# Last residual of a two-layer decoder step: tiles 4 and 5 scaled and added on GpSimd, tile 3 on VectorE, six stores of the result

## The chip, the cores and the metric

One core of one Trainium2 chip. The metric is the device time of one execution, in microseconds; the median of three runs of the kernel before is 1430.1.

## The reference

The program is one inference step of a small decoder: 256 new prompt tokens and 8 x 8 sampled tokens, together 320 columns (TOK), go through two layers of 1024 channels. Each layer is a pair of half-step SwiGLU networks around a token mixer (gated delta rule in the first, latent attention in the second), with an RMSNorm before and after each of the six sub-layers. The change touches only the very end, the post-norm and the residual of the last sub-layer:

```python
x = x + 0.5 * rmsnorm(swiglu(rmsnorm(x, norm_pre[layer, 2]), ffn_in[layer, 1], ffn_out[layer, 1]), norm_post[layer, 2])
# rmsnorm: y * rsqrt(mean(y * y) + EPS) * g
```

and the store of that x, the outputs y_prompt and y_sample. Everything is float32.

## The kernel before

Activations lie transposed: channel on the partition, token on the free axis. The 1024 channels are KT = 8 tiles m of 128 x 320, each tile one slice `x[:, m, :]` of the residual (the profile calls it parx_sb) and one `y[:, m, :]`. Weights stream in as chunks, are split in a high and a low part by ScalarE (L263) and VectorE (L270), and TensorE multiplies all through the kernel. The order of work is written out by hand for each engine; engines wait for each other on counting semaphores.

The last sub-layer is stage s = 5. Its output product (L380 to L382) leaves tile m in PSUM bank m. What follows on each engine:

ScalarE (`post_act`, L389) squares every bank, and copies banks 1, 3 and 5, times the gain, to y (L392). VectorE (`post_dve_sum`, L482) sums the squares and copies banks 0, 2 and 4 to y (L495). Banks 6 and 7 stay in PSUM. TensorE sums over partitions with a matrix of ones, in two halves of 160 tokens, into banks 1 and 3 (L679 to L683). ScalarE makes the reciprocal root r_post from each half with Ln and Exp (L408, L410), and raises `rpost_ready` after each half.

Then comes the last residual, x + y * r_post, over four engines. VectorE (`last_residual_dve`, L438) scales tiles 0 and 1, and 2 and 3, by the first half of r_post, then the same by the second half; then it scales tiles 4 and 5 whole (one operation of 640 columns), adds them to x (640 columns), forms y for 6 and 7 out of PSUM, gain and r_post (L461), and adds these two tiles one by one (L447). TensorE (`last_sums_pe`, L427) adds tiles 0 to 3: it multiplies x by the identity into the bank (L433) and y by the identity on top (L436); for float32 each such product is two passes. ScalarE copies these four banks into x (L414).

The output y_t is stored in five pieces: ScalarE's queue issues tiles 0 and 1 (L417) and 2 and 3 (L419), SyncE's queue issues tiles 4 and 5, then 6, then 7 (L3035), each after the semaphore of its producer. SyncE then waits for all of them. GpSimd has nothing to do in this stage; the last it did was the products of the SwiGLU (`ffn_pool`, L837).

Of the kernel before, what the change touches and what calls it, by code (L numbers as in the profile page):

```python
# [32 lines left out]
TOK = SEQ + NSMP  # L33
KT = D_MODEL // P
# [89 lines left out]
def build(nc, io):  # L124
    ctx = ExitStack()
    with ctx:
# [4 lines left out]
        def sem(name):  # L131
            return ctx.enter_context(nc.semaphore(name))
# [8 lines left out]
        x = par_x[:, XOFF:XOFF + KT * TOK].rearrange("p (k t) -> p k t", k=KT)  # L141
# [5 lines left out]
        y = sb("y", [P, KT, TOK])  # L147
# [6 lines left out]
        r_post = sb("r_post", [P, TOK])  # L154
        r_pre = sb("r_pre", [P, TOK])
        gx = sb("gx", [P, TOK])
        HALF = [slice(0, TOK // 2), slice(TOK // 2, TOK)]
# [231 lines left out]
        def post_act(act, s, c_last, gcol):  # L389

            def copy(m):
                act.activation(y[:, m, :], bank[m][:, 0:TOK], ACT.Identity, scale=gcol(m)).then_inc(y_copied_act, 1)  # L392

            for m in range(KT):
                if m < KT - 1:
                    act.wait_ge(y_done, (KT - 1) * s + m + 1)
                else:
                    act.wait_ge(chunk_done, c_last + 1)
                if m >= 4:
                    act.wait_ge(y_summed, NSUM * s + max(1, m - 4))  # L400
                for t in (HALF if m == KT - 1 else [slice(0, TOK)]):
                    act.activation(sqx[m % 4][:, t], bank[m][:, t], ACT.Square).then_inc(y_squared, 1)
                if m in (1, 3, 5):
                    copy(m)
            for n, t in enumerate(HALF):
                st = STATS[f"post{s}"] - 1 + n
                act.wait_ge(stat_done, st)
                act.activation(r_post[:, t], bank[2 * n + 1][:, t], ACT.Ln, scale=1 / D_MODEL, bias=epsc[:, :]).then_inc(ln_done, 1)  # L408
                act.wait_ge(ln_done, st)
                act.activation(r_post[:, t], r_post[:, t], ACT.Exp, scale=-0.5).then_inc(rpost_ready, 1)  # L410
            if s == 5:
                for m in LAST_PE:
                    act.wait_ge(y_done, (KT - 1) * (s + 1) + LAST_PE.index(m) + 1)
                    act.activation(x[:, m, :], bank[m][:, 0:TOK], ACT.Copy).then_inc(y_copied_act, 1)  # L414
                    if m == LAST_PE[1]:
                        act.wait_ge(y_copied_act, 5 * s + 3 + 2)
                        act.dma_start(io["y_t"][:, 0:2, :], x[:, 0:2, :]).then_inc(third_then_out, 16)  # L417
                act.wait_ge(y_copied_act, 5 * s + 3 + 4)
                act.dma_start(io["y_t"][:, 2:4, :], x[:, 2:4, :]).then_inc(third_then_out, 16)  # L419
                return  # L420
            copy(6)
            copy(7)


        LAST_PE = (0, 1, 2, 3)

        def last_sums_pe(pe):  # L427
            s = 5
            pe.wait_ge(y_copied, 3 * (s + 1))
            for m in (0, 2, 1, 3):  # L430
                if m == 1:
                    pe.wait_ge(ln_done, STATS["post5"])
                pe.matmul(bank[m][:, 0:TOK], ident, x[:, m, :], start=True, stop=False)  # L433
            for m in LAST_PE:
                pe.wait_ge(y_scaled, (KT + 1) * s + (3 if m < 2 else 4))
                pe.matmul(bank[m][:, 0:TOK], ident, y[:, m, :], start=False, stop=True).then_inc(y_done, 1)  # L436

        def last_residual_dve(dve):  # L438
            s = 5
            gcol = half(5)  # L440
            wide = lambda t: r_post[:, t].unsqueeze(1).to_broadcast([P, 2, t.stop - t.start])

            def scale(m, t):
                dve.tensor_tensor(y[:, m:m + 2, t], y[:, m:m + 2, t], wide(t), ALU.mult).then_inc(y_scaled, 1)

            def add(lo, hi):
                dve.tensor_tensor(x[:, lo:hi, :], x[:, lo:hi, :], y[:, lo:hi, :], ALU.add).then_inc(x_ready, hi - lo)  # L447

            dve.wait_ge(y_copied, 3 * (s + 1))
            dve.wait_ge(y_copied_act, 5 * s + 3)  # L450
            dve.wait_ge(rpost_ready, 2 * s + 1)
            scale(0, HALF[0])
            scale(2, HALF[0])
            dve.wait_ge(rpost_ready, 2 * s + 2)
            scale(0, HALF[1])
            scale(2, HALF[1])
            scale(4, slice(0, TOK))
            dve.wait_ge(y_scaled, (KT + 1) * s + 5)
            add(4, 6)
            for m in (6, 7):  # L460
                dve.scalar_tensor_tensor(out=y[:, m, :], in0=bank[m][:, 0:TOK], scalar=gcol(m), in1=r_post[:, :],  # L461
                                         op0=ALU.mult, op1=ALU.mult).then_inc(y_scaled, 1)
            for m in (6, 7):
                dve.wait_ge(y_scaled, (KT + 1) * s + m)
                add(m, m + 1)

        def rsqrt_act(act, stat, n, out, inv_n, out_sem):

# [363 lines left out]
        def ffn_pool(pool, f):  # L832
            with pool.Fori(0, HT // 2) as j:
                for i in range(2):
                    pool.wait_ge(g_ready, HT * f + i + 1 + 2 * j)
                    pool.wait_ge(u_ready, HT * f + i + 1 + 2 * j)
                    pool.tensor_tensor(f_gu[i][:, :], f_g[i][:, :], f_u[i][:, :], ALU.mult).then_inc(gu_ready, 1)  # L837
# [140 lines left out]

        S0_AT = {(1, "d1"): ("keys", 0), (1, "d2"): ("keys", 1), (2, "d1"): ("queries", 0), (2, "d2"): ("queries", 1)}

        s0_landed, gate_copied = sem("s0_landed"), sem("gate_copied")
        gate_act, gate_dve, gate_pe, cols_ready = sem("gate_act"), sem("gate_dve"), sem("gate_pe"), sem("cols_ready")
        pre_ready, conv_first, conv_step, conv_exp = sem("pre_ready"), sem("conv_first"), sem("conv_step"), sem("conv_exp")
        silu_step, sig_ready, qkv_ready, pad_ready = sem("silu_step"), sem("sig_ready"), sem("qkv_ready"), sem("pad_ready")
# [2004 lines left out]
        @block.sync  # L2989
        def _(sp):  # L2990
            n1, n2 = XOFF + 2 * TOK, XOFF + 4 * TOK
            sp.dma_start(par_x[:, 0:n1], io["par_x"][:, 0:n1]).then_inc(x_landed, 16)
            sp.dma_start(par_x[:, n1:n2], io["par_x"][:, n1:n2]).then_inc(x_rest[0], 16)
            sp.dma_start(par_x[:, n2:], io["par_x"][:, n2:]).then_inc(x_rest[1], 16)
            for q in (2, 3):
                for c in range(2):
                    load_quarter(sp, c, q)
            sp.dma_start(raw_third[:, :], io["wts"][2, :, :]).then_inc(third_then_out, 16)
            sp.dma_start(con[:, :], io["consts"]).then_inc(con_landed, 16)
            sp.dma_start(pages[:, :], io["page_table"]).then_inc(con_landed, 16)  # L3000
            sp.dma_start(ctok_flat[:, 2 * KV_LORA - 64:], io["gw"]).then_inc(con_landed, 16)
            load_chunk(sp, 3)
            with sp.Fori(1, (BASE["uk"] - 2) // 2) as j:
                for i in range(2):
                    load_chunk(sp, 2 + i, j)
            load_chunk(sp, BASE["uk"] - 1)
            load_chunk(sp, BASE["uk"])
            sp.wait_ge(con_landed, 48)
            sp.wait_ge(chunk_done, BASE["dq"] + 2)
            load_pages(sp, 0, aland, 0)  # L3010
            load_pages(sp, 0, aland, 1)
            load_chunk(sp, BASE["uk"] + 1)
            sp.wait_ge(qn_hi, 4)
            sp.wait_ge(qn_lo, 4)
            sp.wait_ge(chunk_done, BASE["kv"] + 1)
            for i in range(2, NUN):
                load_pages(sp, 0, aland, i)
                load_plain(sp, 0, spland, i - 2)
            for i in range(NUN - 2, NUN):
                load_plain(sp, 0, spland, i)  # L3020
            sp.wait_ge(n_scores, NP)
            sp.wait_ge(s_done, NUN)
            sp.wait_ge(pv_page, QP * (NUN - 1))
            load_chunk(sp, BASE["uk"] + 2)
            sp.wait_ge(pv_page, QP * NUN)
            sp.wait_ge(s_ot, NP)
            load_chunk(sp, BASE["uk"] + 3)
            load_chunk(sp, BASE["uk"] + 4)
            c = BASE["uk"] + 5
            with sp.Fori(0, (NCHUNK - c) // 2) as j:  # L3030
                for i in range(2):
                    load_chunk(sp, c + i, j)
            for lo, hi in ((4, 6), (6, 7), (7, 8)):
                sp.wait_ge(x_ready, 5 * KT + hi - 4)
                sp.dma_start(io["y_t"][:, lo:hi, :], x[:, lo:hi, :]).then_inc(third_then_out, 16)  # L3035
            sp.wait_ge(third_then_out, 16 + 16 * 5)

        @block.gpsimd
        def _(pool):
# [37 lines left out]
                load_plain(pool, 1, ppland, i)  # L3077
            second_high_pool(pool, BASE["ffn3"] + 1)
            ffn_pool(pool, 3)
            pool.wait_ge(ss_out, 16 * NG)  # L3080
            pool.wait_ge(ss1_out, 16 * NG)
            pool.wait_ge(sp_out, 16 * NG)
# [202 lines left out]
```

## Time and profile before

| what | value |
|---|---|
| runs, median of 3 (lowest, highest) | 1430.1 us (1429.97, 1430.61) |
| profiled execution, span (the only time it gives) | 1428.4 us |
| TensorE busy | 1412.2 us, 99% |
| VectorE busy | 889.8 us, 62% |
| ScalarE busy | 742.7 us, 52% |
| GpSimd busy | 161.9 us, 11% |
| data moved by DMA | 221.01 MB, mean 155 GB/s |

The span runs from the first to the last instruction of the profiled execution. Busy shares are means over it; in the last residual TensorE and VectorE are both nearly always busy and GpSimd is idle. All times in the rows below are microseconds from the start of the span, unless marked ns. PE is TensorE, DVE VectorE, ACT ScalarE, POOL GpSimd, SP SyncE; a q behind the name is the engine's queue of DMA issues.

### The profile page before, as it was taken

How to read it: one execution, taken by the hardware profiler on the slowest of the kernel's cores; microseconds unless marked ns; L12 is line 12 of the kernel's file. 1: busy time of each engine (PE TensorE's matmuls, PEld its weight loads, DVE VectorE, ACT ScalarE, POOL GpSimd, SP SyncE). 2: the span in 40 equal slices, each digit the busy share in tenths (PEclk: the TensorE clock that was granted, in tenths of full speed). 3: DMA queues.
4: the chain of work that ended last, by engine and by line, in shares of the span. 5: the costliest groups of instructions: out<-in, count | busy, mean ns of one | idle time of the engine just before them, and what ended most of it. 6: DMA issues, size and time to landing. Idle time of an engine off the chain costs nothing.

```text
span 1428.4 us, 29450 instructions
## 1 busy us (share of the span) xinstructions
PE 1412.2 (99%) x11003; PEld 1346.2 (94%) x11003; DVE 889.8 (62%) x1480; ACT 742.7 (52%) x1218; POOL 161.9 (11%) x229
## 2 busy tenths in 40 slices
PE   9999999999999999999999999999999999999998
PEld 9999999999888999999999999999877699999998
DVE  6655535999888675554376555349755548655534
ACT  6555424788646565553265555346533346555423
POOL 0111000010110011110011111001144201111000
PEclk9999999999999999999999999999999999999999
DMA  6444443344242254444434444444599643444441
GB/s 242 163 149 151 153 154 136 119 152 146 100 155 98 89 177 147 147 147 148 147 119 166 154 151 147 154 147 150 187 293 285 212 156 118 169 152 150 147 147 67
DMA packets 50776, 221.01 MB, mean 155 GB/s; under 512 B 6705, under 2 KB 23474, under 8 KB 28802
## 3 DMA queue, kind: packets, MB, share of 16 engines
q1 hardware_dynamic: 38882, 189.07, 38.0%
q0 software_dynamic: 6192, 24.64, 5.2%
q10 hardware_dynamic: 5616, 6.16, 1.3%
q8 instruction: 54, 0.88, 0.3%
q14 instruction: 32, 0.26, 0.1%
HBM read 213.07 MB, written 6.77 MB: 154 GB/s over the span
## 4 chain that ended last, share of the span: by engine, by line
PE 94%; DVE 3%; ACT 2%; issue 1%; DMA 0%; DVEq 0%
PE psum L283 16%; PE psum L287 15%; PE psum L282 15%; PE psum L381 8%; PE psum L380 8%; PE psum L382 8%; PE psum L2681 2%; PE psum L2639 2%; PE psum L309 1%; PE psum L300 1%; PE psum L325 1%; PE psum L304 1%; PE psum L2510 1%; PE psum L311 1%; PE psum L315 1%; PE psum L1553 1%
## 5 line engine op out<-in xcount | busy, mean ns | idle before, releaser
L270 DVE TENSOR_TENSOR w_lo<-raw,w_hi 128x2048 fp32r<-128x2048 f32 x159 | 368.6, 2318 | 290.5 <-ACT w_hi L263 290.4
L263 ACT ACTIVATE w_hi<-raw 128x2048 fp32r<-128x2048 f32 x155 | 296.7, 1914 | 351.7 <-PE psum L382 207.8
L282 PE MATMUL psum<-h_hi,w_hi 128*128 128x320 f32 x1504 | 446.0, 310 | 0.0
L283 PE MATMUL psum<-h_lo,w_hi 128*128 128x320 f32 x1504 | 444.1, 309 | 0.0
L282 PEld LDWEIGHTS psum<-h_hi,w_hi 128*128 128x128 f32 x1504 | 282.1, 188 | 2.6 <-issue 1.3
L283 PEld LDWEIGHTS psum<-h_lo,w_hi 128*128 128x128 f32 x1504 | 283.4, 188 | 0.5
L287 PE MATMUL psum<-h_hi,w_lo 128*128 128x320 f32 x1504 | 251.3, 309 | 0.0
L287 PEld LDWEIGHTS psum<-h_hi,w_lo 128*128 128x128 f32 x1504 | 228.3, 188 | 0.3 <-DVE w_lo L270 0.3
L380 PE MATMUL psum<-hid_hi,w_hi 128*128 (+1 forms) x704 | 217.4, 309 | 0.0
L381 PE MATMUL psum<-hid_lo,w_hi 128*128 (+1 forms) x704 | 217.4, 309 | 0.0
L382 PE MATMUL psum<-hid_hi,w_lo 128*128 (+1 forms) x704 | 217.4, 309 | 0.0
L837 POOL TENSOR_TENSOR f_gu<-f_g,f_u 128x320 f32<-128x320 f32 x88 | 77.5, 881 | 567.1 <-DVE f_u L795 567.1
L380 PEld LDWEIGHTS psum<-hid_hi,w_hi 128*128 128x128 f32 x704 | 132.4, 188 | 0.0
L381 PEld LDWEIGHTS psum<-hid_lo,w_hi 128*128 128x128 f32 x704 | 132.4, 188 | 0.0
L382 PEld LDWEIGHTS psum<-hid_hi,w_lo 128*128 128x128 f32 x704 | 132.4, 188 | 0.0
L756 ACT ACTIVATE hid_hi<-f_h 128x320 f32 (+1 forms) x88 | 41.5, 472 | 128.1 <-DVE f_h L800 128.1
L794 DVE TENSOR_TENSOR f_g<-psum,r_pre 128x320 f32<-128x320 f32 x88 | 43.1, 490 | 72.2 <-PE psum L287 72.2
L803 DVE TENSOR_TENSOR hid_lo<-f_h,hid_hi 128x320 f32 (+1 forms) x88 | 43.3, 492 | 66.8 <-ACT hid_hi L756 66.8
L752 ACT ACTIVATE f_e<-f_e,onec 128x320 f32<-128x320 f32 x88 | 49.6, 563 | 2.9
L800 DVE TENSOR_TENSOR f_h<-f_gu,f_e 128x320 f32<-128x320 f32 x88 | 42.5, 483 | 5.0 <-ACT f_e L754 5.0
L480 POOL CAST w_hi<-raw 128x2048 fp32r<-128x2048 f32 x5 | 9.5, 1908 | 299.2 <-PE psum L382 299.2
L754 ACT ACTIVATE f_e<-f_e 128x320 f32<-128x320 f32 x88 | 41.6, 472 | 2.8
(459 smaller groups left out, 1957.4 us busy)
## 6 DMA issues: line engine op xcount, KB each, us to landing
raw<-wts SPq DMA_DIRECT2D x161, 1024.0 KB, 4.8
h_plain<-cache_t POOLq DMA_DIRECT2D x44, 160.0 KB, 3.7
h_plain<-cache_t SPq DMA_DIRECT2D x44, 160.0 KB, 3.7
arena<-s POOLq DMA_DIRECT2D x4, 1024.0 KB, 7.2
sgs<-arena POOLq DMA_DIRECT2D x4, 1024.0 KB, 4.6
marena<-cache_t POOLq DMA_DIRECT2D x20, 160.0 KB, 4.0
marena<-cache_t SPq DMA_DIRECT2D x20, 160.0 KB, 3.6
raw<-cache_c SPq DMA_DIRECT2D x16, 128.0 KB, 4.2
```

The costliest lines, as they stand in the source:

```text
L263: act.activation(w_hi[c0 % 2][:, :], raw_of(c0, pair)[:, :], ACT.Copy).then_inc(hi_ready, 1)
L270: eng.tensor_tensor(w_lo[c0 % 2][:, :], raw_of(c0, pair)[:, :], w_hi[c0 % 2][:, :].bitcast(F32), ALU.subtract).then_inc(lo_ready, 1)
L282: pe.matmul(outs[n], wtile(w_hi, c0, tile0 + n * K + k), src_hi(k), start=(k == 0), stop=False)
L283: pe.matmul(outs[n], wtile(w_hi, c0, tile0 + n * K + k), src_lo(k), start=False, stop=False)
L287: last = pe.matmul(outs[n], wtile(w_lo, c0, tile0 + n * K + k), src_hi(k), start=False, stop=(k == K - 1))
L380: pe.matmul(o, wtile(w_hi, c0, 2 * m + kk), s_hi, start=(start and kk == 0), stop=False)
L381: pe.matmul(o, wtile(w_hi, c0, 2 * m + kk), s_lo, start=False, stop=False)
L382: last = pe.matmul(o, wtile(w_lo, c0, 2 * m + kk), s_hi, start=False, stop=(stop and kk == 1))
L752: act.activation(f_e[i][:, :], f_e[i][:, :], ACT.Ln, bias=onec[:, :]).then_inc(d_ready, 1)
L794: dve.tensor_tensor(f_g[i][:, :], gate, r_pre[:, :], ALU.mult).then_inc(g_ready, 1)
L803: dve.tensor_tensor(one(hid_lo), f_h[i][:, :], one(hid_hi).bitcast(F32), ALU.subtract) \
L837: pool.tensor_tensor(f_gu[i][:, :], f_g[i][:, :], f_u[i][:, :], ALU.mult).then_inc(gu_ready, 1)
```

## The change

Tiles 4 and 5 go from VectorE to GpSimd: the new `last_residual_pool` scales each of them in two halves of 160 tokens, as the halves of r_post become ready, and then adds each to x. TensorE and ScalarE keep tiles 0, 1 and 2 instead of 0 to 3; tile 3, still scaled together with tile 2, is added by VectorE. The stores become six: ScalarE's queue issues 0 and 1, then 2 alone, then, after a wait for GpSimd, 4 and 5; SyncE's queue issues 3, 6 and 7. GpSimd's progress is counted on a semaphore that was done with (`gate_copied`, at 2 by then), under the name `last_pool`.

```diff
@@ ScalarE, end of post_act @@
-                act.wait_ge(y_copied_act, 5 * s + 3 + 4)
-                act.dma_start(io["y_t"][:, 2:4, :], x[:, 2:4, :]).then_inc(third_then_out, 16)
+                act.wait_ge(y_copied_act, 5 * s + 3 + 3)
+                act.dma_start(io["y_t"][:, 2:3, :], x[:, 2:3, :]).then_inc(third_then_out, 16)
+                act.wait_ge(last_pool, 2 + 6)
+                act.dma_start(io["y_t"][:, 4:6, :], x[:, 4:6, :]).then_inc(third_then_out, 16)
@@ TensorE @@
-        LAST_PE = (0, 1, 2, 3)
+        LAST_PE = (0, 1, 2)
-            for m in (0, 2, 1, 3):
+            for m in (0, 2, 1):
@@ VectorE @@
-            def add(lo, hi):
-                dve.tensor_tensor(x[:, lo:hi, :], x[:, lo:hi, :], y[:, lo:hi, :], ALU.add).then_inc(x_ready, hi - lo)
+            def add(m):
+                dve.tensor_tensor(x[:, m, :], x[:, m, :], y[:, m, :], ALU.add).then_inc(x_ready, 1)
...
             scale(0, HALF[1])
             scale(2, HALF[1])
-            scale(4, slice(0, TOK))
-            dve.wait_ge(y_scaled, (KT + 1) * s + 5)
-            add(4, 6)
+            dve.wait_ge(y_scaled, (KT + 1) * s + 4)
+            add(3)
             for m in (6, 7):
                 dve.scalar_tensor_tensor(out=y[:, m, :], in0=bank[m][:, 0:TOK], scalar=gcol(m), in1=r_post[:, :],
                                          op0=ALU.mult, op1=ALU.mult).then_inc(y_scaled, 1)
             for m in (6, 7):
-                dve.wait_ge(y_scaled, (KT + 1) * s + m)
-                add(m, m + 1)
+                dve.wait_ge(y_scaled, (KT + 1) * s + m - 1)
+                add(m)
@@ GpSimd, new, called after ffn_pool(pool, 3) @@
+        def last_residual_pool(pool):
+            s = 5
+            pool.wait_ge(y_copied, 3 * (s + 1))
+            pool.wait_ge(y_copied_act, 5 * s + 3)
+            for n, t in enumerate(HALF):
+                pool.wait_ge(rpost_ready, 2 * s + n + 1)
+                for m in (4, 5):
+                    pool.tensor_tensor(y[:, m, t], y[:, m, t], r_post[:, t], ALU.mult).then_inc(last_pool, 1)
+            for m in (4, 5):
+                pool.wait_ge(last_pool, 2 + m - 1)
+                pool.tensor_tensor(x[:, m, :], x[:, m, :], y[:, m, :], ALU.add).then_inc(last_pool, 1)
@@ SyncE @@
-            for lo, hi in ((4, 6), (6, 7), (7, 8)):
-                sp.wait_ge(x_ready, 5 * KT + hi - 4)
-                sp.dma_start(io["y_t"][:, lo:hi, :], x[:, lo:hi, :]).then_inc(third_then_out, 16)
-            sp.wait_ge(third_then_out, 16 + 16 * 5)
+            for n, m in enumerate((3, 6, 7)):
+                sp.wait_ge(x_ready, 5 * KT + n + 1)
+                sp.dma_start(io["y_t"][:, m, :], x[:, m, :]).then_inc(third_then_out, 16)
+            sp.wait_ge(third_then_out, 16 + 16 * 6)
```

## Rows read from the trace of the kernel before

**Rows 1.** Head of the page

```profile
span 1428.4 us, 29450 instructions
```

**Rows 2.** Chain of waits, end of the kernel: start us, length us, what

```profile
1419.79 2.44 DVE y L444 x5
...
1422.33 0.83 DVE parx_sb L447
...
1423.15 0.92 DVE y L461 x2
...
1424.07 0.40 DVE parx_sb L447
```

**Rows 3.** Timeline of VectorE: start us, us, engine, line, operation, tiles

```profile
1419.79 0.49 DVE L444 TENSOR_TENSOR y<-y,r_post 128x320 f32<-128x320 f32 x1 [1.25 <-ACT r_post L410]
...
1421.01 1.22 DVE L444 TENSOR_TENSOR y<-y,r_post 128x320 f32<-128x320 f32 x2
...
1423.99 0.88 DVE L447 TENSOR_TENSOR parx_sb<-parx_sb,y 128x320 f32<-128x320 f32 x2
```

**Rows 4.** Timeline of ScalarE and its DMA queue, last residual

```profile
1420.14 0.34 ACT L410 ACTIVATE r_post<-r_post 128x160 f32<-128x160 f32 x1
...
1422.40 0.97 ACT L414 ACTIVATE parx_sb<-psum 128x320 f32<-128x320 f32 x2 [1.93 <-PE psum L436]
...
1423.41 0.37 ACTq L417 DMA_DIRECT2D y_t<-parx_sb  x1
...
1423.82 0.77 ACT L414 ACTIVATE parx_sb<-psum 128x320 f32<-128x320 f32 x2 [0.45 <-PE psum L436]
...
1424.62 0.35 ACTq L419 DMA_DIRECT2D y_t<-parx_sb  x1
```

**Rows 5.** Timeline of TensorE, last residual

```profile
1419.51 2.32 PE L433 MATMUL psum<-parx_sb,con 128*128 128x320 f32 x8
1421.66 2.32 PE L436 MATMUL psum<-y,con 128*128 128x320 f32 x8
```

**Rows 6.** Timeline of SyncE's DMA queue, first and last store

```profile
1423.18 0.35 SPq L3035 DMA_DIRECT2D y_t<-parx_sb  x1
...
1424.90 0.44 SPq L3035 DMA_DIRECT2D y_t<-parx_sb  x1
```

**Rows 7.** Windows of the final stores; last columns: DMA share, GB/s

```profile
1424.00:1424.10 0.10, 0.00 (x0) 0.00 (x0) 0.10 (x2) 0.10 (x1) 0.00 (x0) 1.00 0.57 205
...
1424.10:1427.50 3.40, 0.00 (x0) 0.00 (x0) 0.77 (x2) 0.49 (x2) 0.00 (x0) 0.88 0.97 378
...
1427.60:1427.70 0.10, 0.00 (x0) 0.00 (x0) 0.00 (x0) 0.00 (x0) 0.00 (x0) 0.50 0.01 0
```

**Rows 8.** Timeline of GpSimd, two instructions beside VectorE

```profile
288.77 2.96 POOL L1344 COPY tmp<-tmp 8x320 f32<-8x320 f32 x1
...
292.90 1.04 POOL L1347 TENSOR_TENSOR y<-y 8x320 f32<-8x320 f32 x1
```

**Rows 9.** Timeline of VectorE in the same stretch

```profile
289.14 2.27 DVE L270 TENSOR_TENSOR w_lo<-raw,w_hi 128x2048 fp32r<-128x2048 f32 x1
...
292.02 1.17 DVE L1309 SCALAR_TENSOR_TENSOR arena<-arena,parx_sb 128x344 f32<-128x344 f32 x1
...
293.12 1.19 DVE L1309 SCALAR_TENSOR_TENSOR arena<-arena,parx_sb 128x344 f32<-128x344 f32 x1
```

**Rows 10.** VectorE's line 1309 over the kernel (min/median/max ns)

```profile
L1309 DVE SCALAR_TENSOR_TENSOR arena<-arena,parx_sb x72: 557/567/1185, 264.4 to 364.0; 128x344 f32<-128x344 f32 x72
```

**Rows 11.** Groups of GpSimd by form: count, busy us, mean ns

```profile
L837 POOL TENSOR_TENSOR f_gu<-f_g,f_u 128x320 f32<-128x320 f32 x88 | 77.5, 881 | 567.1 <-DVE f_u L795 567.1
...
L2048 POOL TENSOR_TENSOR arena<-con,arena 128x128 f32<-128x128 f32 x2 | 0.9, 458 | 1.3 <-DVE arena L1894 1.3
```

**Rows 12.** Timeline, GpSimd beside a VectorE instruction that reads PSUM

```profile
374.58 0.73 POOL L2048 TENSOR_TENSOR arena<-con,arena 128x256 f32<-128x256 f32 x1 [2.74 <-DVE arena L1894]
374.75 0.47 DVE L1857 TENSOR_TENSOR arena<-psum,arena 128x128 f32<-128x128 f32 x2
```

More of the change, by code:

```diff
@@ L979, in build @@
         S0_AT = {(1, "d1"): ("keys", 0), (1, "d2"): ("keys", 1), (2, "d1"): ("queries", 0), (2, "d2"): ("queries", 1)}
-        s0_landed, gate_copied = sem("s0_landed"), sem("gate_copied")
+        s0_landed, gate_copied = sem("s0_landed"), sem("gate_copied_then_last")
+        last_pool = gate_copied
         gate_act, gate_dve, gate_pe, cols_ready = sem("gate_act"), sem("gate_dve"), sem("gate_pe"), sem("cols_ready")
@@ L3079, in _ @@
             ffn_pool(pool, 3)
+            last_residual_pool(pool)
             pool.wait_ge(ss_out, 16 * NG)
```

## The prediction

> **What bounds the kernel now.** I read the head of the page first: one core, a span of 1428.4 us [rows 1]. The median of the three runs shown is 1430.1 us, 1.7 us more; the profile gives no other time of its execution, so I work out the change of the span and add 1.7. Everything touched lies in the last 9 us. There I read the chain of waits, the timelines of the engines, and narrow windows over the last transfers.
>
> The chain runs through VectorE: five scales, one double add, two operations on PSUM, two single adds [rows 2]. The last add ends at 1424.87 1423.99 + 0.88, [rows 3], SyncE issues its store at 1424.90 [rows 6]. But the windows say something else about what comes last. The DMA engines start 0.57 into the slice 1424.00 to 1424.10 (so at about 1424.05), are 97% busy until 1427.50, and are done at about 1427.6 [rows 7]. All eight tiles of y_t (8 x 128 x 320 x 4 bytes = 1.31 MB) go through in these 3.55 us, at 378 GB/s without a hole: 0.444 us per tile. The last store was issued at 1424.90 and could have had data moving 0.86 us later (the first took 1424.05 - 1423.18 = 0.87, [rows 6, 7]), at 1425.77, and been done at 1426.2; it is done at 1427.6 because it stands behind the others. So what decides the end is **when the first store starts**, as long as the later ones follow fast enough, and not the last add. After the last byte come 0.8 us to the end of the span, which stay.
>
> **VectorE's part.** Removed: the scale of tiles 4 and 5 (640 columns, from 1421.40 to 1422.23) and their double add (1422.33, 0.83 long; the next instruction follows 0.74 after its start, at 1423.07). Added: one single add, of tile 3. Four scales have a pitch of 0.405 (1419.79 to 1421.01 is three of them, [rows 3]), so undisturbed the fourth ends at 1421.49, add(3) starts at 1421.58 (the same 0.10 wait as before the double add) and ends at 1422.06; the operations on PSUM begin at 1421.99 instead of 1423.07, and all that follows is 1.08 us earlier: last add done at 1423.79.
>
> **TensorE and ScalarE.** Two passes for x and two for y of tile 3 go (0.27 each, 2.15 between the first of line 433 and the first of line 436, for eight, [rows 5]). The six x passes would be done at 1419.51 + 6 x 0.27 = 1421.13, so the first y pass is no longer held by them but by the scales: y_scaled 3 (the third scale, before 1421.08) and, for tile 2, the fourth. From the start of the y passes to the first ScalarE copy it is 1422.40 - 1421.66 = 0.74, from there to the end of the second copy 0.97, then the issue [rows 4, 5]. The third copy comes 0.41 after that issue and takes 0.44 [rows 4]; then a single-tile store, then the store of 4 and 5, which waits for GpSimd. Each issue costs ScalarE's queue 0.35 to 0.37; nothing of ScalarE's stands behind the new wait.
>
> **GpSimd's part.** Four half-tile products (160 columns) and two adds (320). A 320-column two-input operation takes 0.88, 256 columns 0.73, 128 columns 0.46 [rows 11, 12]; that is 2.1 ns per column, so 160 columns come to 0.53, an estimate from these rows. Undisturbed: start 1419.80, two products to 1420.86, the second half of r_post has been there since 1420.48 [rows 4], two more to 1421.92, two adds to about 1423.75. ScalarE's queue would not reach the store of 4 and 5 before 1424.16, so it would be hidden.
>
> **But the two engines are not undisturbed.** In one earlier stretch GpSimd and VectorE both read two operands, or one, from SBUF at once [rows 8, 9]. GpSimd's copy, recorded from 288.77, lasts 2.96 us and ends 0.32 after VectorE's split (289.14 + 2.27 = 291.41) does. Then they alternate: VectorE's line 1309, which takes 0.56 elsewhere [rows 10], takes 1.17 and 1.19; the first ends at 293.19, GpSimd's at 293.94, 0.75 later; the second of VectorE at 294.31, 0.37 later. A full mutual exclusion, one instruction each in turn. Where VectorE reads one operand from PSUM, neither is stretched: GpSimd's 256 columns take 0.73, VectorE's two of 128 take 0.47 [rows 12].
>
> Every scale and every single add of the last residual has both operands in SBUF; the two operations on tiles 6 and 7 read PSUM. So I put them in turn. After GpSimd ends, a VectorE operation of 320 columns ends 0.345 later (0.37 less 24 columns); after VectorE ends, GpSimd's 320 columns end 0.75 later, and 160 columns between 0.40 (0.75 less 160 x 2.1 ns) and 0.53 (its free time); I take 0.42, near the row. Who begins? GpSimd was recorded 0.37 us ahead of VectorE at 288.77, and VectorE's instruction went through first; both are released here by the same r_post half, so I take VectorE first.
>
> Scale 1 ends 1420.27; GpSimd 1420.69; scale 2 1421.04; GpSimd 1421.46; scale 3 1421.80; GpSimd 1422.22; scale 4 1422.57; GpSimd 1422.99; add(3) 1423.33; GpSimd's add(4) 1424.08. VectorE's two PSUM operations lie beside that, to about 1424.2; then add(6) to 1424.67, GpSimd's add(5) to 1425.42, add(7) to 1425.77. So each of four scales costs VectorE 0.77 rather than 0.40, and the last add is 0.9 **later** than before.
>
> The stores: tile 3 is issued at 1423.36, data from 1424.22. Tiles 0 and 1: y passes from 1421.85, first copy 1422.59, issue 1423.60, ready 1424.46, before the first store (0.44) is through. Tile 2: third copy from 1424.01, issue 1424.47, ready 1425.33, before 1425.55. Tile 6 issued 1424.70; tiles 4 and 5 1425.45, ready 1426.31, against a queue busy until 1426.44; tile 7 issued 1425.80, ready 1426.66. Without a hole, then: 1424.22 + 8 x 0.444 = 1427.77, against 1427.6. **The sum is +0.17 us**: span 1428.6, runs 1430.3. Of the six stores, four have rows of 1280 bytes where there were two; the windows do not tell the two kinds apart, and the extra issue lies beside transfers; I take 0, with -0.05 and +0.15 as bounds. The 160-column bounds (0.40, 0.53) over the four turns before add(3) give -0.1 and +0.4.
>
> [...]
>
> **Rivals.**
> *No exclusion here* (the products are short and slip in between, or VectorE keeps its turns). For it: GpSimd is slower, so in a queue without turns VectorE could run its four scales in a row. Against it: the alternation of [rows 8, 9]. Tile 3 is issued at 1422.08, data 1422.94 to 1423.38; tiles 0 and 1: y passes from 1421.15, issue 1422.90, data from 1423.76; seven tiles at 0.444 end at 1426.87, so -0.75 us: 1429.35. A mixed case, where some turns are lost, lies between.
>
> *GpSimd begins* (the slower side). Place: 1419.8, the first product ahead of the first scale. It is decided by who has the turn at the release; if GpSimd is first, every scale stands behind one more product: scale 1 ends 1420.67, scale 3 1422.20, scale 4 1422.97, and add(4), whose product is long done, goes before add(3), which ends 1424.07. Tiles 0 and 1 are issued at 1424.0, the first data move at 1424.86, the end is 1428.4: +0.8 us, 1430.9. [...]
>
> *A cost of GpSimd that no row has* (its first instruction after a long idleness, its wake by ScalarE): its store is the only one late. The other six tiles keep the transfers busy until 1424.22 + 6 x 0.444 = 1426.88, so it costs from the point at which GpSimd's last add ends after 1426.0 (0.87 earlier), and one us of delay more is one us of time; only a delay above 3 us past that point leaves the bound of no change. Against it: GpSimd's last products earlier start and run like the first ones [rows 11].
>
> *The change does nothing outside the tail*: code, buffers and queues of the first 1410 us are the same, so no gain or loss is looked for there.
>
> **How the numbers follow.** In turn, VectorE first: 0.5. No or partial exclusion, faster by 0.3 to 0.8 us: 0.25. GpSimd first, +0.8: 0.2. Unpriced GpSimd cost: 0.05. The likeliest alone would be 1429.9 to 1430.8; with the two others, and the 0.6 us by which the three runs shown differ, 1429.3 to 1431.2. What can be told from no change is 0.2%, 2.9 us; all three main cases lie well inside: faster 0.01, same 0.96, slower 0.03.
>
> **What would show it.** VectorE's four scales at a pitch near 0.77 us and not 0.40, GpSimd's products between them, the last add of VectorE near 1425.8, GpSimd's 0.35 before or after it; first DMA work near 1424.2 and no hole until 1427.8. Scales at 0.40 prove the first rival; a GpSimd product that ends before the first scale does, with the first scale near 0.9 us long, the second. A hole in the DMA share between 1424.5 and 1427 would break the step that the transfers alone set the end.

## The result, and the profile after

The changed kernel is **slower**, by 0.4%: 1435.75 us in the median of six runs (1435.36 to 1436.89), against 1430.49 for six runs of the kernel before; ratio 1.0038, 95% interval 1.0028 to 1.0048. The prediction said 1430.3, a range of 1429.3 to 1431.2, and no change that can be told. One execution each of e1, e5 and e9 below took about two to two and a half times the usual time; the medians hold it, the ratios leave it out. The profiled execution has a span of 1434.1 us where before had 1428.4 [rows 1], 5.7 us more.

What is said of the engines ahead of the prediction can be read from the trace of before: line 263 runs 156 times on ScalarE (median 1.9 us) and line 270 160 times on VectorE (2.3 us), TensorE is busy 99% of the span, the two passes of a product are the x8 of [rows 5] for four tiles, and from 1419.8 to 1424.9 TensorE is busy 4.18 of the 5.10 us, VectorE 4.97 and GpSimd none.

The work itself went nearly as forecast. The timeline of VectorE in the changed kernel (start us, us, engine, line, operation; compare [rows 3]):

```profile
1419.85 0.49 DVE L446 TENSOR_TENSOR y<-y,r_post 128x320 f32<-128x320 f32 x1 [1.25 <-ACT r_post L410]
...
1420.26 0.81 DVE L446 TENSOR_TENSOR y<-y,r_post 128x320 f32<-128x320 f32 x1
...
1420.99 0.81 DVE L446 TENSOR_TENSOR y<-y,r_post 128x320 f32<-128x320 f32 x1
...
1422.56 0.69 DVE L449 TENSOR_TENSOR parx_sb<-parx_sb,y 128x320 f32<-128x320 f32 x1
...
1423.17 1.00 DVE L462 SCALAR_TENSOR_TENSOR y<-psum,halfpost,r_post 128x320 f32<-128x320 f32 x2
...
1424.10 1.45 DVE L449 TENSOR_TENSOR parx_sb<-parx_sb,y 128x320 f32<-128x320 f32 x2
```

and of GpSimd, whose rows have no counterpart before:

```profile
1419.88 0.84 POOL L475 TENSOR_TENSOR y<-y,r_post 128x160 f32<-128x160 f32 x1 [77.39 <-ACT r_post L410]
...
1420.68 0.77 POOL L475 TENSOR_TENSOR y<-y,r_post 128x160 f32<-128x160 f32 x1
...
1422.87 1.93 POOL L478 TENSOR_TENSOR parx_sb<-parx_sb,y 128x320 f32<-128x320 f32 x2
```

The first scale takes its usual 0.49; the following ones 0.81 and start 0.73 apart instead of 0.405, since between two of them one of GpSimd's products has its turn. The last add ends at 1425.55, 0.68 after that of before. ScalarE and its queue (compare [rows 4]): two copies, the store of 0 and 1, then, with the third copy between, the stores of 2 and of 4 and 5:

```profile
1422.69 0.98 ACT L414 ACTIVATE parx_sb<-psum 128x320 f32<-128x320 f32 x2 [2.16 <-PE psum L438]
...
1423.70 0.37 ACTq L417 DMA_DIRECT2D y_t<-parx_sb  x1
...
1424.58 0.35 ACTq L419 DMA_DIRECT2D y_t<-parx_sb  x1
...
1424.98 0.47 ACTq L421 DMA_DIRECT2D y_t<-parx_sb  x1
```

The transfers (narrow windows; last two columns DMA share and GB/s, compare [rows 7]):

```profile
1423.90:1424.10 0.20, 0.00 (x0) 0.00 (x0) 0.20 (x2) 0.00 (x0) 0.20 (x2) 1.00 0.00 0
1424.10:1427.80 3.70, 0.00 (x0) 0.00 (x0) 1.45 (x3) 0.44 (x1) 0.69 (x1) 0.89 0.93 354
1427.80:1434.10 6.30, 0.00 (x0) 0.00 (x0) 0.00 (x0) 0.00 (x0) 0.00 (x0) 0.50 0.00 0
```

Nothing moves before 1424.1, then the DMA engines are 93% busy to 1427.8: 0.1 us later at the start and 0.2 to 0.25 us later at the end than before. And then 6.3 us in which no engine computes and nothing is transferred; before, 0.8 us followed the last byte. That is 5.5 of the 5.7 us. What lies in it is on no engine's timeline of computing instructions. It is in the rows of line 126, where the program closes its block. In both traces each of the five engines has one DRAIN there. VectorE's begins before its last add has ended and is over 0.05 us after it (at 1424.93 before, 1425.60 after); how long GpSimd's goes on after its last work is read below. Behind the DRAINs stand the EVENT_SEMAPHORE rows. In the changed kernel all of them lie between 1433.91 and 1434.10, though the DRAINs of the other four engines are over by 1428.39; before, they lie between 1428.17 and 1428.36, behind SyncE's DRAIN. I call them the barrier. The rows are engine's queue, operation, count: duration ns min/median/max, first and last start. The changed kernel:

```profile
L126 POOLq DRAIN  x1: 10597/10597/10597, 1423.3 to 1423.3; - x1
...
L126 SPq COMPARE_BRANCH  x1: 38/38/38, 1428.2 to 1428.2; - x1
...
L126 SPq DRAIN  x1: 7/7/7, 1428.4 to 1428.4; - x1
...
L126 SPq EVENT_SEMAPHORE  x1: 17/17/17, 1434.0 to 1434.0; - x1
```

The kernel before:

```profile
L126 POOLq DRAIN  x1: 9512/9512/9512, 1342.0 to 1342.0; - x1
...
L126 SPq COMPARE_BRANCH  x1: 38/38/38, 1428.0 to 1428.0; - x1
...
L126 SPq DRAIN  x1: 7/7/7, 1428.1 to 1428.1; - x1
...
L126 SPq EVENT_SEMAPHORE  x1: 17/17/17, 1428.3 to 1428.3; - x1
```

The reader is to see two things. SyncE, which waits for the last store, is through at nearly the same time in both (1428.1 and 1428.4). And **GpSimd's DRAIN takes 9.5 us before and 10.6 us after**. Before, it starts at 1342.0, while the last product of the SwiGLU still runs, and is over at 1351.5, 9.08 us after that product, beside 77 us in which GpSimd has nothing else to do. After, GpSimd works until 1422.87 + 1.93 = 1424.80, and the DRAIN, begun at 1423.27, ends at 1433.87, 9.08 us after that work. The barrier opens at 1434.0. The view of waits names TensorE's queue for SyncE's wait of 5.7 us there, but the DRAIN that ended last is GpSimd's: TensorE's was over at 1423.78, and the steps of all engines in the barrier lie within 0.2 us, after 1433.9 (us in total, times, longest us):

```profile
SPq L126 <- PEq L126: 5.7, 1, 5.7
SPq L126 <- DMA y_t<-parx_sb: 2.2, 1, 2.2
```

### The profile page after: what moved, and what is told of

Read it like the earlier page. It is cut to its first block, busy times and chain, and to the rows that moved or that the text cites. A ratio compares the mean times of both kernels' runs of the same rounds, so it can differ in the third digit from the quotient of the medians.

```text
span 1434.1 us, 29447 instructions
## 1 busy us (share of the span) xinstructions
PE 1411.6 (98%) x10999; PEld 1345.5 (94%) x10999; DVE 891.4 (62%) x1479; ACT 742.1 (52%) x1217; POOL 167.0 (12%) x235
## 4 chain that ended last, share of the span: by engine, by line
PE 94%; DVE 3%; ACT 2%; issue 1%; DMA 0%; DVEq 0%
PE psum L283 16%; PE psum L287 15%; PE psum L282 15%; PE psum L380 8%; PE psum L381 8%; PE psum L382 8%; PE psum L2695 2%; PE psum L2653 2%; PE psum L309 1%; PE psum L300 1%; PE psum L325 1%; PE psum L304 1%; PE psum L2524 1%; PE psum L311 1%; PE psum L315 1%; PE psum L1567 1%
```

## The experiments

All runs were made beside runs of the kernel before on the same chip; ratios are to those. "Tail" is the time from the start of the first scale of VectorE to the end of the span, in the profiled execution: it leaves out what differs in the 1419 us ahead (the first scale starts anywhere from 1419.3 to 1421.4 in these profiles). Before it is 8.57 us, in the changed kernel 14.25.

**e1, the DRAIN left out of the change.** The block is opened with `no_gpsimd_drain=True`. In the trace of this run, line 126 has one DRAIN each of SyncE, ScalarE, VectorE and TensorE, and none of GpSimd.

```diff
-        block = ctx.enter_context(nc.Block())
+        block = ctx.enter_context(nc.Block(no_gpsimd_drain=True))
```

> The change, with GpSimd's DRAIN at the end of the program left out (all its transfers are waited for by semaphores before). Theory A: the 5.3 us are the DRAIN of GpSimd, 10.6 us long from 1423.3 to 1433.9, that the final barrier waits for, and nothing else. Then the span ends 0.2 to 0.3 us after SyncE's arrival (1428.4 in the changed kernel): span 1428.6, runs 1430.3 us, GpSimd's arrival at the barrier before SyncE's. Theory B: something else of GpSimd at the end (its late adds, a cost of its first instruction after idleness, the barrier itself) costs it: runs stay at 1435.7 us.

Measured: 1430.44 us against 1429.92 for the kernel before, ratio 1.0004 (0.9995 to 1.0013); span 1428.9, tail 8.86. Some rows of line 126 in this run:

```profile
L126 SPq EVENT_SEMAPHORE  x2: 17/17/17, 1428.7 to 1428.9; - x2
...
L126 POOLq EVENT_SEMAPHORE  x2: 17/17/17, 1428.7 to 1428.8; - x2
...
L126 SPq DRAIN  x1: 7/7/7, 1428.6 to 1428.6; - x1
```

GpSimd's step in the barrier starts right behind SyncE's at 1428.7 (1428.75 and 1428.71). Theory A holds, B falls: GpSimd's work, its first instruction after a long wait and its late adds together cost no more than the 0.3 us by which this tail is longer than that of before. The edit does not leave everything else as it was: each engine but GpSimd now has two EVENT_SEMAPHORE steps where it had one. That the DRAIN matters and not this is shown by e4, where each of them has one step as before, and the span is 1428.1.

**e2, the same in the kernel before.** Same edit.

> The kernel before, with GpSimd's final DRAIN left out. Theory A: there it runs from 1342.0 to 1351.5, beside 77 us in which GpSimd has nothing to do, so it costs nothing: within 0.5 us of the kernel before (1430.1 to 1430.5). If leaving the DRAIN out saves time in itself (theory C: a shorter barrier), this kernel is faster than before by the same amount as e1 is faster than 1430.3.

Measured: 1429.89 against 1429.92, ratio 1.0001 (0.9992 to 1.0010), span 1428.3. Under cover the DRAIN costs nothing that can be told; theory C falls.

**e3, the kernel before with a late wait on GpSimd and no work.**

```diff
             ffn_pool(pool, 3)
+            pool.wait_ge(rpost_ready, 12)
```

> The kernel before, with one wait added on GpSimd after its last product: for the second half of r_post of the last stage (ready at 1420.5). No work is added. Theory A with a fixed length of the DRAIN from its start: it starts at about 1420.9 and ends at 1430.4, span 1430.7 against 1428.4, so runs are 2.2 to 2.4 us slower than before (1432.5). Theory D: the long DRAIN is the price of the instructions GpSimd has just run: after 77 us of waiting it is short, runs as before (1430.3).

Measured: 1431.58 against 1429.92, ratio 1.0013 (1.0004 to 1.0022); span 1429.9.

```profile
L126 POOLq EVENT_SEMAPHORE  x2: 17/17/17, 1429.7 to 1429.8; - x2
...
L126 POOLq DRAIN  x1: 9052/9052/9052, 1420.6 to 1420.6; - x1
...
L126 SPq DRAIN  x1: 7/7/7, 1428.0 to 1428.0; - x1
```

The DRAIN starts at 1420.58, takes 9.05 us, and GpSimd reaches the barrier at 1429.67, 1.6 us after SyncE. A single wait, with nothing computed behind it, made the kernel 1.7 us slower. The 2.2 to 2.4 of the expectation was too much: the DRAIN starts 0.2 us after r_post is ready, not 0.4, and with no work in front of it lasts 9.05 us, not 9.5. D falls: the price does not belong to instructions just run.

**e4, the change with one more DRAIN where GpSimd is idle.**

```diff
             ffn_pool(pool, 3)
+            pool.drain()
             last_residual_pool(pool)
```

> The change, with one more DRAIN on GpSimd before its last residual, where it is idle for 77 us. If the DRAIN clears up something that gathers over the kernel (its transfers), the early one takes the 9.5 us under cover, the final one is short, and runs come to 1430.3 us. If every DRAIN of GpSimd costs its 9 us (fixed price), there are two long ones and runs stay at 1435.7 us.

Measured: 1429.9 against 1429.92, ratio 1.0001 (0.9992 to 1.0010), span 1428.1, tail 8.77. The extra DRAIN (line 3094) and the final one:

```profile
L3094 POOLq DRAIN  x1: 9855/9855/9855, 1341.2 to 1341.2; - x1
...
L126 POOLq DRAIN  x1: 1582/1582/1582, 1422.8 to 1422.8; - x1
...
L126 SPq DRAIN  x1: 7/7/7, 1427.9 to 1427.9; - x1
```

The extra one takes the 9.9 us, of which 9.08 come after the product in front of it, at 1341.2 to 1351.1, under cover. The final one is 1.58 long and only waits for the last add (1422.36 + 1.92 = 1424.28, end at 1424.36). So the price is owed by something that gathers, and is paid once. **One instruction gives back the whole loss.**

**e5 and e6, what gathers.** The same extra DRAIN at two other places: in e5 behind GpSimd's last page transfer, in e6 between its first 12 transfers and the 98 small ones of the attention.

```diff
 # e5
+            pool.drain()
             second_high_pool(pool, BASE["ffn3"] + 1)
 # e6
+            pool.drain()
             second_high_pool(pool, BASE["dq"] + 1)
```

> The change, with the extra DRAIN of GpSimd set right behind its last page transfer, so between it and the final DRAIN lie GpSimd's cast, its 22 products of the last SwiGLU and the last residual, but no transfer. Theory T (the 9.1 us clear up after GpSimd's 110 transfers): the final DRAIN ends at once after the last add, as in e4; runs 1429.9 to 1430.3 us. Theory P (they are owed by compute instructions, or by code loaded since): the final DRAIN is again several us longer than the wait for the last add and runs lie at 1433 to 1435.7 us.

> The change, with the extra DRAIN set between the two large groups of GpSimd's transfers: 12 transfers (9.5 MB, 1472 packets) lie before it, 98 small ones (15.1 MB, 4720 packets) behind it. What is left for the final DRAIN after the last add tells the unit. By count of transfers: 98/110 of 9.08 us, 8.1 us, runs 1434.8 us, the early one 1.0 us. By packets: 4720/6192, 6.9 us, runs 1433.6. By bytes: 15.1/24.6, 5.6 us, runs 1432.3. All of it fixed once per kernel: 9.1 us here and a short early one, 1435.7 us, or the reverse.

Measured: e5 1430.58 against 1430.26, ratio 1.0002 (0.9992 to 1.0011). e6 1435.01, ratio 1.0035 (1.0022 to 1.0048). Early and final DRAIN of e5:

```profile
L3092 POOLq DRAIN  x1: 9620/9620/9620, 1136.2 to 1136.2; - x1
...
L126 POOLq DRAIN  x1: 1595/1595/1595, 1423.6 to 1423.6; - x1
```

and of e6:

```profile
L3072 POOLq DRAIN  x1: 1846/1846/1846, 884.1 to 884.1; - x1
...
L126 POOLq DRAIN  x1: 9608/9608/9608, 1423.1 to 1423.1; - x1
```

The timeline of GpSimd in e6 has its last adds, at whose end (1424.65) the rest of the DRAIN begins:

```profile
1422.73 1.92 POOL L478 TENSOR_TENSOR parx_sb<-parx_sb,y 128x320 f32<-128x320 f32 x2
```

In e5 the final DRAIN is as short as in e4 although the cast and 22 products lie between (last add until 1425.09, DRAIN until 1425.16): theory T. In e6 what is left after the last add is 1423.14 + 9.61 - 1424.65 = 8.09 us, and of the early one, behind the product that ends at 884.89, 1.07 us. Taken together, with the number of transfers that GpSimd has issued since its last DRAIN:

| transfers since the last DRAIN | DRAIN beyond the last work | run |
|---|---|---|
| 0 | 0.07 to 0.08 us | e4, e5, e7, final |
| 12 (large) | 1.07 us | e6, early |
| 98 (small) | 8.09 us | e6, final |
| 110 | 9.05 to 9.08 us | before, after, e3; e4, e5, e7 early |

That is 0.07 us and 0.082 us for each transfer, by count: 98 give 8.09 where packets would have given 6.9 and bytes 5.6. Nor is it the reading of page numbers (TENSOR_LOAD), which goes with 96 of the 98: the first 12 have none, and cost as much each. It is no wait for data either. In e5 the last two transfers landed at 1137.7 and 1139.7, inside the early DRAIN, which ends 9.06 us after the last issue; in the kernel before all had landed over 200 us earlier, and it is 9.08. What the engine does for each transfer is in no trace, and stays open.

**e7, GpSimd's operations without reads.** The change with the early DRAIN, and in `last_residual_pool`:

```diff
-    pool.tensor_tensor(y[:, m, t], y[:, m, t], r_post[:, t], ALU.mult).then_inc(last_pool, 1)
+    pool.memset(y[:, m, t], 0.0).then_inc(last_pool, 1)
-    pool.tensor_tensor(x[:, m, :], x[:, m, :], y[:, m, :], ALU.add).then_inc(last_pool, 1)
+    pool.memset(x[:, m, :], 0.0).then_inc(last_pool, 1)
```

> e4 (early DRAIN), with GpSimd's four products and two adds replaced by memsets of the same regions, which read nothing from SBUF; tiles 4 and 5 of y_t are then zero. Exclusion by reads: VectorE's four scales go back from a pitch of 0.73 us to 0.40, its last add ends near 1423.8 instead of 1425.5, the first data of y_t move at 1422.9, the span is 0.7 us shorter than that of e4. If any access of GpSimd shuts VectorE out, or if the pitch of 0.73 comes from something else in the changed order of work, the scales stay above 0.6.

Measured: 1429.77 against 1430.26, ratio 0.9999 (0.9989 to 1.0008); span 1427.9, tail 8.04 against 8.77 in e4. VectorE's scales and last adds, and two of GpSimd's memsets between them:

```profile
1419.89 1.70 DVE L446 TENSOR_TENSOR y<-y,r_post 128x320 f32<-128x320 f32 x4 [1.24 <-ACT r_post L410]
...
1422.95 0.88 DVE L449 TENSOR_TENSOR parx_sb<-parx_sb,y 128x320 f32<-128x320 f32 x2
...
1420.63 0.41 POOL L475 MEMSET y<- 128x160 f32 x2 [0.32 <-ACT r_post L410]
```

Four scales in 1.70 us again, the pitch 0.405, with GpSimd active beside them; the last add ends at 1423.83, 3.94 us after the first scale instead of 5.70. With GpSimd's reads gone the exclusion is gone: pitch 0.405 against 0.73. Its price is less sure: the tail is 0.73 us shorter, but that is two single profiles, and the ratios of e4 and e7 do not tell them apart. Nor is it the whole shift: the first data move 1.2 us sooner after the first scale than in e4, and nearly 0.5 us of that is lost again, most of it in a pause of the transfers behind the first tile (1423.6 to 1424.0), as in e8 below.

**e8, e9, e10: without GpSimd, the first store earlier.** VectorE adds tile 3 behind its four scales and keeps 4 and 5.

```diff
 # e8, VectorE (GpSimd's part removed; stores 3, 4:6, 6, 7 on SyncE, 0:2 and 2 on ScalarE)
+            add(3, 4)
             scale(4, slice(0, TOK))
...
             add(4, 6)
 # e9: SyncE's queue issues 3, 0, 1, 4:6, 6, 7 one by one, ScalarE 2
 # e10: e9 with tiles 2 and 3 scaled first (stores 3, 2, 0, 4:6, 6, 7 on SyncE, 1 on ScalarE),
 # TensorE and ScalarE in the order
+        LAST_PE = (2, 0, 1)
```

> A version without GpSimd in the last residual: VectorE adds tile 3 right after its four scales, then scales and adds tiles 4 and 5 itself as in the kernel before; TensorE and ScalarE keep 0 to 2; six stores (SyncE 3, 4 and 5, 6, 7; ScalarE 0 and 1, 2). GpSimd's DRAIN is back under cover. If the first store decides the end: first data at 1422.9 against 1424.05, last add 0.4 us later than before (1425.3), transfers end at 1426.9, span 0.7 us shorter than before, runs 1429.3 us. If the last add decides: 0.4 us slower than before, 1430.4 us.

> e8 with seven stores: SyncE's queue issues 3, 0, 1, then 4 and 5, 6, 7, each as its producer is done; ScalarE issues 2. In e8 the transfers start at 1423.13 but pause for half a microsecond after tile 3, since tiles 0 and 1 are issued together after the second copy. If the first store and the holes after it set the end: the pause goes, transfers end 0.3 us earlier than in e8, 0.85 us before the end of before, tail from the first scale to the end of the span 7.7 us (before 8.57, e8 8.02), runs about 1429.2. If it is the last add: as e8.

> e9 with tiles 2 and 3 ahead of 0 and 1: scales in the order (2,3), (0,1) for each half, TensorE and ScalarE take tile 2 first, SyncE stores 3, 2, 0, then 4 and 5, 6, 7, ScalarE stores 1. By the transfers, the first data move 2.8 us after the first scale (e8: 3.1) and nothing is missing behind, the end comes 0.3 us before that of e9: tail 7.4 us, runs 1429.0. By the last add (5.3 us after the first scale in e8, 5.1 here): its store is issued at 5.1, data 0.87 later, 0.44 long, and 0.75 to the end of the span, so 7.2 us is the floor.

Measured: e8 1429.53 against 1430.26, ratio 0.9995 (0.9986 to 1.0004), tail 8.02. e9 1430.30 against 1430.51, 0.9999 (0.9991 to 1.0008), tail 7.93. e10 1429.77 against 1430.51, 0.9995 (0.9986 to 1.0004), tail 7.80. VectorE's timeline in e8:

```profile
1420.02 1.70 DVE L444 TENSOR_TENSOR y<-y,r_post 128x320 f32<-128x320 f32 x4 [1.25 <-ACT r_post L410]
...
1421.75 0.49 DVE L447 TENSOR_TENSOR parx_sb<-parx_sb,y 128x320 f32<-128x320 f32 x1
...
1424.74 0.89 DVE L447 TENSOR_TENSOR parx_sb<-parx_sb,y 128x320 f32<-128x320 f32 x2
```

and windows of its transfers (last two columns DMA share, GB/s):

```profile
1423.00:1423.60 0.60, 0.25 (x1) 0.00 (x0) 0.52 (x1) 0.19 (x1) 0.00 (x0) 1.00 0.69 260
1423.60:1424.05 0.45, 0.00 (x0) 0.00 (x0) 0.45 (x2) 0.42 (x1) 0.00 (x0) 1.00 0.06 17
1424.05:1427.30 3.25, 0.00 (x0) 0.00 (x0) 1.58 (x4) 0.02 (x1) 0.00 (x0) 0.78 0.92 353
```

Tile 3 moves from 1423.1, then the DMA engines pause, then they are busy to 1427.3. The last add ends 5.61 us after the first scale where before it was 5.08, and still the tail is 0.55 us shorter: in the kernel before, the last add is not what sets the end, as the prediction's first part said. In e9 and e10 the pause goes, and the gain is smaller than expected (tail 7.93 and 7.80, not 7.7 and 7.4): now the DMA engines wait for work, and the last add sets the end. From its end to the end of the span it is 2.32 us in both; in e8 it was already down to 2.41, so only 0.1 us was left to gain from closing the pause. The 7.2 us of the expectation for e10 took 5.1 us to the last add, where it is 5.48, and 2.1 behind it. VectorE's timeline in e10:

```profile
1421.43 1.70 DVE L441 TENSOR_TENSOR y<-y,r_post 128x320 f32<-128x320 f32 x4 [1.25 <-ACT r_post L410]
...
1426.03 0.89 DVE L444 TENSOR_TENSOR parx_sb<-parx_sb,y 128x320 f32<-128x320 f32 x2
```

and the window from its first to its last data:

```profile
1424.40:1428.50 4.10, 0.26 (x1) 0.00 (x0) 2.51 (x5) 0.64 (x2) 0.00 (x0) 0.97 0.85 320
```

The DMA engines are 85% busy in it, where they were 97% in the 3.4 us of [rows 7]. Last add at 1426.91, end of span at 1429.2: 2.3 us for issue, transfer and closing, against 3.5 before. e8 and e10 are the best versions and beat the changed kernel by 6 us; against the kernel before their intervals include 1, and only the tails of single profiles speak for them.

## Why the prediction was wrong

By its steps:

- *VectorE and GpSimd in turn.* Right. VectorE's operation ends 0.35 after GpSimd's (0.345 forecast). GpSimd's 160 columns end 0.38 after VectorE's, where 0.42 was taken and 0.40 was the lower bound; a pitch of 0.73, not 0.77. In e7, where GpSimd reads nothing, the pitch is 0.405.
- *VectorE first.* Right at the first scale (1419.85 against 1419.88, and 0.49 long). Wrong at add(6): GpSimd's add(5) was first, and add(6) took 1.05. It did no harm, since the last add ends at 1425.55 anyway, before the forecast 1425.77.
- *The transfers set the end of the work.* Right, and the time of the end (1427.8, 1427.77 forecast) by two small misses that cancel: the first data move at about 1424.14, not 1424.22, and the eight tiles then take longer than the 3.55 us carried over from before. By the packets' records they take 3.58 to 3.59 us in the three traces with the old order of stores (before, e2, e3) and 3.72 to 3.73 us in the five with that of the change (after, e1, e4, e5, e6). So the term for the extra store that was put at 0, with -0.05 and +0.15 as bounds, is +0.14. (The 0.57 of [rows 7] is the busy share of its slice and not the place of the start in it; by the packets' records the start was 1424.04, so nothing hangs on it.) e1 and e4 show what the forecast sum gives when nothing else is in the way: tails 0.2 to 0.3 us longer than before (0.17 forecast) and runs of 1430.44 and 1429.9 us beside 1429.92 for the kernel before (1430.3 forecast, beside 1430.1).
- *"After the last byte come 0.8 us to the end of the span, which stay."* **This step failed**, and alone made the difference: they became 6.3. I took the 0.8 us for a property of the last store, when they were the later of two arrivals at a barrier, and SyncE's was the later one only because GpSimd had come 77 us earlier. The row that would have told me stood in the trace of before: the DRAIN of 9512 ns at line 126. I read the queues' rows for DMA issues only, and costed the moved instructions one by one, but not what stands behind them on GpSimd: its end.
- *The rival of an unpriced cost of GpSimd* had the right engine, 1 chance in 20 and the wrong path: I let it act only through its store. With 9.08 us after the last add (forecast for 1425.42), the same addition would have given 1434.5 + 0.2, a span of 1434.7 and runs of 1436.4 us. The 0.6 us above what was measured is GpSimd's last add, which ended at 1424.80 and not at 1425.42.
- *GpSimd begins; no exclusion.* Both fell at 1419.9: scale 1 is undisturbed, scales 2 to 4 are not.

## What to carry to other kernels

Before work is given to an idle engine near the end of a kernel, ask what that engine still owes after its last instruction, and read the closing rows of every engine, not only those that compute: a cost that is hidden because the engine was idle comes into view with the first late instruction on it, even a mere wait (e3: 1.7 us). If GpSimd has issued many transfers, try one DRAIN where it is idle: in e4, after 110 transfers, the final DRAIN then ended 0.07 us after the last add instead of 9.08, and the ratio to the kernel before fell from 1.0038 to 1.0001. And where stores follow each other without a hole, look at the first one's time and not only at the last one's: in e8 the last add ends 0.53 us later after the first scale than before (5.61 against 5.08), and the tail is 0.55 us shorter. That went on here until the last add came so late that the DMA engines had to wait for it (85% busy in e10 against 97% before; 2.32 us from the last add to the end in e9 and e10).

## What the hardware did that I had not expected

GpSimd's DRAIN costs 0.07 us and 0.082 us for each transfer that its queue has issued since the last DRAIN, by count and not by size, even 200 us after they have landed: 9.08 us for 110 here. In this kernel 96 of the 224 page loads go through that queue, so by this count, as an estimate, the price would grow by 0.082 us with every page on that queue (not tried). And the mutual exclusion of VectorE and GpSimd goes by turns here, one instruction each, even when VectorE has several in a row ready: a product of 160 columns on GpSimd is recorded as 0.77 us and ends 0.38 us after VectorE's instruction does.
